# Modulation by rows of 128 outputs in the down phases of three networks, with narrower splits of the down weights

## The chip, the cores and the metric

The kernel runs on one core of one Trainium2 chip. A core has TensorE (matmul), VectorE, ScalarE and GpSimd, each with its own queue of instructions, and SyncE, which here only issues DMAs. The metric is device time in microseconds from first to last instruction as the runtime measures it. Three executions of the kernel before took 2091.39, 2093.84 and 2096.69 us.

## The reference

Two transformer blocks over x of 512 tokens by 1024 features, all in fp32. The first has a SwiGLU network, a mixer of attention, convolution and memory attention (mixA), and a second SwiGLU network. The second block has two layers; each has a mixer (mixB, an attention over selected keys; mixC, a short convolution) and a SwiGLU network of its own. In all: network 0, mixA, network 1, mixB, network 2, mixC, network 3. The second block's layers are modulated by a vector c:

```
c_act = jax.nn.silu(c)
for i in range(DEPTH_2):
    mod = c_act @ ada_w[i] + ada_b[i]              # (1, 6*1024)
    sh1, sc1, g1, sh2, sc2, g2 = split(mod, 6)
    h = _rmsnorm(x, norm1_g[i]) * (1.0 + sc1) + sh1
    x = x + g1 * mixer(h)
    h = _rmsnorm(x, norm2_g[i]) * (1.0 + sc2) + sh2
    x = x + g2 * _swiglu(h, w_gate[i], w_up[i], w_down[i])
```

ada_w is 2 x 1024 x 6144, 50.3 MB in fp32, read once and used for one vector only. It yields 12288 numbers, the tile modc of 128 partitions by 96 columns. From it come geff0 to geff3 (the norms' gains times 1 + scale), the shifts and the gates. They are first needed in the down phase of network 1.

## The kernel before, in words

**Matmuls.** Features lie on partitions, the 512 tokens on the free axis. Every fp32 matrix is held as a high and a low part (w_hi, w_lo and h_hi, h_lo), and each product is three matmuls, high x high, low x high, high x low (function product, L823 to L825), each 128x128 by 128x512.

**Jobs and the ring.** Weights come tile by tile, one tile a job, through a ring of four places. SyncE loads w_raw; ScalarE copies it to w_hi (split, L1392); VectorE subtracts to w_lo (split, L1917), or GpSimd does for most of the mixers' tiles (L720). Splits run LEAD = 3 jobs ahead of TensorE: in step s of a phase the engines split job s + 3. ScalarE's copy waits until TensorE has left the ring's place, VectorE's waits for ScalarE's, SyncE's next load for VectorE's.

**A network** has an up phase of 44 jobs (gate and up tiles of 1024 columns, 24 matmuls each) and a down phase of 32 jobs in four rounds of eight. A down job is a quarter of one output tile, of 6, 6, 5 or 5 blocks of 128 columns (DOWN_CUTS), though splits always work on all 1024 columns of a place. After every fourth job VectorE adds the result to x (update_x, L1939), ScalarE squares it, VectorE sums the squares (L1928) and splits the raw input of the next norm (raw_low, L1946).

**Modulation before.** It runs in the up phases of networks 0, 1 and 2, eight steps each of 512 outputs. For a step GpSimd loads four pieces of 512 KB of ada_w into the two places of ada_raw (ada_load, L689). VectorE takes the contraction over partitions and columns: one tensor_scalar and seven scalar_tensor_tensor into ada_sum (modulate), a transpose and a reduce (ada_partial), and GpSimd sends 8 KB through DRAM and back (ada_across), after which VectorE forms the total (ada_total).

**End of a down phase.** In the last round the splits are those of the following stage. GpSimd makes mixA's and mixB's low parts. In networks 1 and 2, shift_through (L1957, L1960) multiplies the mixer's first two weight tiles by the shift and sums over columns, eight operations a tile, on VectorE at steps 5 and 6. TensorE's first instruction of the mixer (first_two, L865) waits for the second one's sum, and then for the low part of the mixer's second tile. In network 1 the second tile has 8 columns a block.

Each engine works its queue strictly in order; what stands behind a waiting instruction waits as well.

## Time and profile before

| | |
|---|---|
| median of 3 runs | 2093.84 us |
| the profiled execution | 2091.56 us, span 2089.8 us |
| TensorE busy | 2071.9 us (99%), 10560 matmuls |
| VectorE busy | 1355.4 us (65%) |
| ScalarE busy | 862.9 us (41%) |
| GpSimd busy | 307.9 us (15%) |
| chain that ended last | PE 91%, DVE 6%, ACT 1% |
| DMA | 243.39 MB, mean 116 GB/s |
| granted TensorE clock | 1.00 |

In the profile PE is TensorE, DVE VectorE, ACT ScalarE, POOL GpSimd, SP SyncE; L1917 is line 1917 of the kernel. Matmuls overlap, and their ends are modelled: one of 512 columns is shown with 390 ns, but they start some 226 ns apart, so TensorE's pace is read from counts, not from busy time. A line may be a helper's: L1917 is every low split of VectorE. The down phases of networks 0, 1 and 2 lie at about 257 to 376, 808 to 928 and 1442 to 1561 us.

### The profile page before, as it was taken

How to read it: one execution, taken by the hardware profiler on the slowest of the kernel's cores; microseconds unless marked ns; L12 is line 12 of the kernel's file. 1: busy time of each engine (PE TensorE's matmuls, PEld its weight loads, DVE VectorE, ACT ScalarE, POOL GpSimd, SP SyncE). 2: the span in 40 equal slices, each digit the busy share in tenths (PEclk: the TensorE clock that was granted, in tenths of full speed). 3: DMA queues.
4: the chain of work that ended last, by engine and by line, in shares of the span. 5: the costliest groups of instructions: out<-in, count | busy, mean ns of one | idle time of the engine just before them, and what ended most of it. 6: DMA issues, size and time to landing. Idle time of an engine off the chain costs nothing.

```text
span 2089.8 us, 30098 instructions
## 1 busy us (share of the span) xinstructions
PE 2071.9 (99%) x10560; PEld 1730.1 (83%) x10560; DVE 1355.4 (65%) x1997; ACT 862.9 (41%) x1346; POOL 307.9 (15%) x369
## 2 busy tenths in 40 slices
PE   9999999999999999999999999999999999999999
PEld 8888888887888888877767888888888888999987
DVE  7666544787576654456997576664456459888832
ACT  6222233567442223334566342223333235455622
POOL 0121400660212221024320202220000000000000
PEclk9999999999999999999999999999999999999999
DMA  5556333330246542333310245642333222233332
GB/s 190 186 184 200 104 105 108 118 105 1 103 160 194 181 159 82 91 110 96 107 46 1 91 141 195 198 159 70 103 102 109 93 98 82 84 111 106 97 97 88
DMA packets 79578, 243.39 MB, mean 116 GB/s; under 512 B 12784, under 2 KB 13424, under 8 KB 79376
## 3 DMA queue, kind: packets, MB, share of 16 engines
q1 hardware_dynamic: 61376, 189.61, 27.8%
q0 software_dynamic: 18128, 52.84, 8.1%
q8 instruction: 42, 0.69, 0.1%
q14 instruction: 32, 0.26, 0.0%
HBM read 235.84 MB, written 2.29 MB: 114 GB/s over the span
## 4 chain that ended last, share of the span: by engine, by line
PE 91%; DVE 6%; ACT 1%; issue 1%; DMA 0%; SPq 0%; ACTq 0%; DVEq 0%
PE ps L823 25%; PE ps L825 25%; PE ps L824 25%; PE ps L919 3%; PE ps L918 3%; PE ps L917 3%; PE ps L1185 2%; DVE ps L2491 1%; PE ps L1167 1%; PE ps L1146 1%; DVE tmp L1960 1%; DVE small L2389 1%; PE ps L1309 0%; DVE ropA L2362 0%; DVE qA L2364 0%
## 5 line engine op out<-in xcount | busy, mean ns | idle before, releaser
L823 PE MATMUL ps<-h_hi,w_hi 128*128 128x512 f32 x1600 | 628.0, 392 | 2.2 <-issue 0.9
L825 PE MATMUL ps<-h_hi,w_lo 128*128 128x512 f32 x1600 | 623.0, 389 | 0.0
L824 PE MATMUL ps<-h_lo,w_hi 128*128 128x512 f32 x1600 | 622.7, 389 | 0.0
L1917 DVE TENSOR_TENSOR w_lo<-w_raw,w_hi 128x1024 fp32r<-128x1024 f32 x300 | 367.4, 1226 | 306.0 <-ACT w_hi L1392 293.6
L1392 ACT ACTIVATE w_hi<-w_raw 128x1024 fp32r<-128x1024 f32 x344 | 361.4, 1052 | 234.9 <-PE ps L825 233.1
L823 PEld LDWEIGHTS ps<-h_hi,w_hi 128*128 128x128 f32 x1600 | 299.6, 187 | 71.7 <-issue 8.2
L825 PEld LDWEIGHTS ps<-h_hi,w_lo 128*128 128x128 f32 x1600 | 299.5, 187 | 63.9
L824 PEld LDWEIGHTS ps<-h_lo,w_hi 128*128 128x128 f32 x1600 | 299.7, 187 | 61.9 <-issue 0.2
L823 PE MATMUL ps<-hid_hi,w_hi 128*128 128x512 f32 x704 | 274.0, 389 | 0.0
L824 PE MATMUL ps<-hid_lo,w_hi 128*128 128x512 f32 x704 | 273.9, 389 | 0.0
L825 PE MATMUL ps<-hid_hi,w_lo 128*128 128x512 f32 x704 | 273.9, 389 | 0.0
L720 POOL TENSOR_TENSOR w_lo<-w_raw,w_hi 128x512 fp32r<-128x512 f32 x100 | 133.6, 1356 | 447.3 <-ACT w_hi L1392 400.3
L1469 ACT ACTIVATE hid_hi<-tmp 128x512 f32 (+1 forms) x66 | 41.7, 632 | 293.2 <-DVE tmp L2097 287.1
L823 PEld LDWEIGHTS ps<-hid_hi,w_hi 128*128 128x128 f32 x704 | 132.1, 188 | 27.7 <-DVE hid_lo L2191 0.3
L824 PEld LDWEIGHTS ps<-hid_lo,w_hi 128*128 128x128 f32 x704 | 132.1, 188 | 27.4
L825 PEld LDWEIGHTS ps<-hid_hi,w_lo 128*128 128x128 f32 x704 | 132.1, 188 | 27.3
L2032 DVE SCALAR_TENSOR_TENSOR ada_sum<-ada_raw,c_act,ada_sum 128x512 f32<-128x512 f32 x168 | 125.9, 749 | 7.4 <-DMA ada_raw<-in_ada_w 3.1
L689 POOL DMA_DIRECT2D ada_raw<-in_ada_w x96 | 52.7, 549 | 393.6 <-DVE ada_sum L2032 372.7
L1466 ACT ACTIVATE tmp<-ps 128x512 f32<-128x512 f32 x62 | 37.1, 598 | 167.2 <-PE ps L825 167.2
L1402 ACT ACTIVATE tmp<-x 128x512 f32 (+1 forms) x56 | 35.3, 630 | 155.7 <-DVE x L1939 155.3
L2097 DVE TENSOR_TENSOR tmp<-tmp,ps 128x512 f32<-128x512 f32 x62 | 42.7, 688 | 78.0 <-PE ps L825 78.0
L2038 DVE TENSOR_TENSOR hid_lo<-tmp,hid_hi 128x512 f32 (+1 forms) x66 | 46.3, 701 | 57.4 <-ACT hid_hi L1469 57.4
(368 smaller groups left out, 2826.0 us busy)
## 6 DMA issues: line engine op xcount, KB each, us to landing
ada_raw<-in_ada_w POOLq DMA_DIRECT2D x96, 512.0 KB, 4.9
w_raw<-in_gate SPq DMA_DIRECT2D x88, 512.0 KB, 4.2
w_raw<-in_up SPq DMA_DIRECT2D x88, 512.0 KB, 3.5
w_raw<-in_down SPq DMA_DIRECT2D x64, 384.0 KB, 3.1
w_raw<-in_down SPq DMA_DIRECT2D x64, 320.0 KB, 2.9
w_raw<-in_w_mix_c SPq DMA_DIRECT2D x24, 512.0 KB, 3.5
w_raw<-in_w_mix_b SPq DMA_DIRECT2D x17, 512.0 KB, 3.5
w_raw<-in_w_mix SPq DMA_DIRECT2D x16, 512.0 KB, 3.5
```

What stands on the lines that cost most here:

```text
L689: pool.dma_start(ada_raw[:, (piece % 2) * 2 * ADA:(piece % 2 + 1) * 2 * ADA], src.rearrange("a p n -> (a p) n")).then_inc(ada_in[piece % 2 ...
L720: low = pool.tensor_tensor(w_lo[:, at:at + WT // 2], w_raw[:, at:at + WT // 2], f32(w_hi[:, at:at + WT // 2]), ALU.subtract)
L823: pe.matmul(dest, s_hi, m_hi, start=first and n == 0, stop=False)
L824: pe.matmul(dest, s_hi, m_lo, start=False, stop=False)
L825: mm = pe.matmul(dest, s_lo, m_hi, start=False, stop=last and n == len(pairs) - 1)
L917: pe.matmul(dest, w_hi[:, cut], m_hi, start=first and c == 0, stop=False, skip_group_check=not first)
L918: pe.matmul(dest, w_hi[:, cut], m_lo, start=False, stop=False, skip_group_check=not first)
L919: mm = pe.matmul(dest, w_lo[:, cut], m_hi, start=False, stop=c == KC // 2 - 1, skip_group_check=not first)
L1392: act.activation(chunk(w_hi, slot, WT), chunk(w_raw, slot, WT), ACT.Copy).then_inc(w_hi_done, 1)
L1917: dve.tensor_tensor(chunk(w_lo, slot, WT), chunk(w_raw, slot, WT), f32(chunk(w_hi, slot, WT)), ALU.subtract).then_inc(w_lo_done, 1)
L2032: dve.scalar_tensor_tensor(ada_sum[:, :], w, c_act[:, k:k + 1], ada_sum[:, :], ALU.mult, ALU.add).then_inc(ada_sum_done, 1)
L2038: dve.tensor_tensor(hid_lo[:, at], chunk(tmp, 2 + u), f32(hid_hi[:, at]), ALU.subtract)\
```

## The change

**Where and how modulation runs.** ada_w comes transposed, so that 128 outputs lie on partitions and the 1024 inputs along the free axis. One tensor_tensor_reduce (ada_row, L2046 after) multiplies a tile of 128x1024 by c_row, sums along the free axis, adds the bias and writes one column of modc; there is no transpose, reduce or trip through DRAM. It is built as two instructions: the multiply-and-sum and a small one that writes the sum. There are 32 rows in the down phase of each of networks 0, 1 and 2. ADA_AT says how many stand ahead of the split in each of a round's eight steps.

**Where the tiles lie.** Three places: slot 0 is the first half of ada_raw; slots 1 and 2, and c_row, lie in chunks 6, 5 and 7 of h_hi and h_lo, whose 512 columns each are free in a down phase until ScalarE writes the next norm's raw input there. So slot 2 is not used after row 25, nor slot 1 after row 29, and ADA_SLOTS ends in 0,1,0,1,0,0. GpSimd loads c_row and then row by row (ada_rows); a load waits until the row that last used its slot is done (ada_done).

**Other parts.** Splits of down weights cover 640 or 768 columns rather than 1024 (down_width). ScalarE's silu of c moves from the start of the kernel to each down phase, on 128x1024 (step 3). GpSimd makes the rope tables in the middle of an up phase, and ScalarE finishes them in step 2 of the down phase rather than ahead of it. The gains are formed in step 6 of the last round. VectorE's four rounds are written out, and one round each at ScalarE's two ends. Places and functions that choose others for network 2 if it were in SEVEN are not in use, as SEVEN is (3,) in both.

```diff
-ADA = 512
-ADA_STEPS = 2 * 6 * D // ADA
-ADA_PER_FFN = 8
+ADA_ROWS = 2 * 6 * KC
+ADA_PER_FFN = ADA_ROWS // 3
+ADA_AT = ((0, 0, 0, 0, 1, 1, 1, 1), (1, 2, 1, 1, 2, 2, 1, 1), (1, 2, 1, 1, 2, 2, 1, 1), (2, 1, 1, 1, 1, 0, 0, 0))
+ADA_SLOTS = (1, 2, 0) * 8 + (1, 2) + (0, 1, 0, 1, 0, 0)
...
+        over = h_over.rearrange("p (s k t) -> p s k t", s=2, k=KC)
+        c_row = over[:, :, KC - 1, :]
+        ada_tile = (ada_raw[:, 0:2 * T].rearrange("p (s t) -> p s t", s=2), over[:, :, KC - 2, :], over[:, :, KC - 3, :])
...
+        def down_width(s, by_parts, ends):
+
+            q = s + LEAD
+            if ends and q >= 8:
+                return WT
+            part = q // 2 if by_parts and q < 8 else q % 4
+            return (DOWN_CUTS[part + 1] - DOWN_CUTS[part]) * P
...
+            def ada_rows(n):
+
+                pool.wait_ge(job_done, first_job[f"ffn{n}"] + UP_JOBS + RING)
+                pool.dma_start(c_row, A["c_row"].rearrange("p (s t) -> p s t", s=2)).then_inc(c_in, 16)
+                for r in range(ADA_PER_FFN):
+                    slot = ADA_SLOTS[r]
+                    if ada_before(r) is not None:
+                        pool.wait_ge(ada_done, n * ADA_PER_FFN + ada_before(r) + 1)
+                    elif slot == 0 and n < 2:
+                        after(pool, a_misc, (("tabA", "tabB")[n], "cos"))
+                    elif slot == 0:
+                        pool.wait_ge(ada_done, n * ADA_PER_FFN)
+                    pool.dma_start(ada_tile[slot], A["ada_w"][n * ADA_PER_FFN + r].rearrange("p (s t) -> p s t", s=2))\
+                        .then_inc(ada_in[slot], 16)
...
+                def ada_row(r):
+
+                    at, slot = n * ADA_PER_FFN + r, ADA_SLOTS[r]
+                    dve.wait_ge(ada_in[slot], 16 * (ada_used(n, r) + 1))
+                    dve.wait_ge(c_ready, n + 1)
+                    dve.tensor_tensor_reduce(ada_tile[slot], ada_tile[slot], c_row, 1.0, col("ada_b", at), ALU.mult, ALU.add,
+                                             modc[:, at:at + 1]).then_inc(ada_done, 1)
...
-                def down(i, last, by_parts=False):
+                def down(i, last, by_parts=False, rows=(0,) * 8):
                     for s in range(8):
+                        for r in range(sum(rows[:s]), sum(rows[:s + 1])):
+                            ada_row(sum(sum(e) for e in ADA_AT[:i]) + r)
...
                         if last and n in (1, 2) and 8 - LEAD <= s < 10 - LEAD:
                             shift_through(2 * n + 1, s - (8 - LEAD))
                         if not (last and (n != 2 and s >= 8 - LEAD or s == 7)):
-                            split(J + UP_JOBS + s + LEAD, i, 8)
+                            split(J + UP_JOBS + s + LEAD, i, 8, down_width(s, by_parts, last))
```

**How the queues change.** VectorE, end of the last round of network 1's down phase, before: four splits, the block around update_x, one split, then shift_through.

```order
L1917 TENSOR_TENSOR w_lo<-w_raw,w_hi 128x1024 x4
L1939 SCALAR_TENSOR_TENSOR x<-ps,flat,x 128x512
L1928 TENSOR_TENSOR ssum<-ssum,tmp 128x512
L1946 SCALAR_TENSOR_TENSOR h_lo<-x,geff,h_hi 128x512
L1917 TENSOR_TENSOR w_lo<-w_raw,w_hi 128x1024
L1957 TENSOR_SCALAR tmp<-w_raw,modc 128x128
L1960 SCALAR_TENSOR_TENSOR tmp<-w_raw,modc,tmp 128x128 x7
L1957 TENSOR_SCALAR tmp<-w_raw,modc 128x8
L1960 SCALAR_TENSOR_TENSOR tmp<-w_raw,modc,tmp 128x8 x7
L1939 SCALAR_TENSOR_TENSOR x<-ps,flat,x 128x512
```

The same round after, from its first instruction to split 6 (rows 26 to 30; an ISA line with an input is the multiply-and-sum, `modc 128x1` its second instruction):

```order
L2046 ISA ada_raw,modc<-ada_raw,h_over,cols 128x1024
L2046 ISA modc 128x1
L2046 ISA h_over,modc<-h_over,cols 128x2x512
L2046 ISA modc 128x1
L1936 TENSOR_TENSOR w_lo<-w_raw,w_hi 128x640
L2046 ISA ada_raw,modc<-ada_raw,h_over,cols 128x1024
L2046 ISA modc 128x1
L1936 TENSOR_TENSOR w_lo<-w_raw,w_hi 128x768
L2046 ISA h_over,modc<-h_over,cols 128x2x512
L2046 ISA modc 128x1
L1936 TENSOR_TENSOR w_lo<-w_raw,w_hi 128x768
```

and from there to shift_through:

```order
L2046 ISA ada_raw,modc<-ada_raw,h_over,cols 128x1024
L2046 ISA modc 128x1
L1936 TENSOR_TENSOR w_lo<-w_raw,w_hi 128x640
L1957 SCALAR_TENSOR_TENSOR x<-ps,flat,x 128x512
L1946 TENSOR_TENSOR ssum<-ssum,tmp 128x512
L1964 SCALAR_TENSOR_TENSOR h_lo<-x,geff,h_hi 128x512
L2046 ISA ada_raw,modc<-ada_raw,h_over,cols 128x1024
L2046 ISA modc 128x1
L1936 TENSOR_TENSOR w_lo<-w_raw,w_hi 128x640
L1975 TENSOR_SCALAR tmp<-w_raw,modc 128x128
L1978 SCALAR_TENSOR_TENSOR tmp<-w_raw,modc,tmp 128x128 x7
```

Six rows now stand in front of shift_through, one of them (row 31) between the last update_x block and split 7. GpSimd's queue at the end of that series, in network 0, before: loads wait for ada_sum, and the trip through DRAM follows.

```order
L689 DMA ada_raw<-in_ada_w 128x1024 [waits ada_sum_done] x2
L696 DMA ada_room<-wi 128x16 [waits ada_done,ada_part_done]
L700 DMA wi<-ada_room 32x4x4 [waits ada_stored]
L700 DMA wi<-ada_room 32x4x4 x3
L729 DMA ada_raw<-in_positions 128x512 [waits ada_sum_done]
L738 CAST ada_raw<-ada_raw 128x512 [waits pos_in]
L740 ISA
```

After (h_over is where slots 1 and 2 lie): rows 24 to 31, each load waiting for an earlier row, then mixA's splits.

```order
L714 DMA h_over<-in_ada_w 128x2x512 [waits ada_done] x2
L714 DMA ada_raw<-in_ada_w 128x1024 [waits ada_done]
L714 DMA h_over<-in_ada_w 128x2x512 [waits ada_done]
L714 DMA ada_raw<-in_ada_w 128x1024 [waits ada_done]
L714 DMA h_over<-in_ada_w 128x2x512 [waits ada_done]
L714 DMA ada_raw<-in_ada_w 128x1024 [waits ada_done] x2
L725 TENSOR_TENSOR w_lo<-w_raw,w_hi 128x512 [waits w_lo_done,w_hi_done]
```

The splits that GpSimd owes to mixA now stand behind the last row's load, which waits for the row before it; before, they stood behind the rope tables.

## Rows read from the trace of the kernel before

**Rows 1.** Stages: busy us (instructions) by engine, clock, DMA share, GB/s.
```profile
50.00:250.00 200.00, 200.00 (x884) 165.62 (x883) 126.72 (x170) 59.42 (x76) 44.28 (x76) 1.00 0.55 178
250.00:370.00 120.00, 120.00 (x532) 99.34 (x530) 53.82 (x56) 43.13 (x50) 13.60 (x11) 1.00 0.33 100
...
1650.00:1700.00 50.00, 50.00 (x222) 41.27 (x221) 23.29 (x28) 12.57 (x15) 0.00 (x0) 1.00 0.29 97
```

**Rows 2.** Waits of TensorE: total us, times, longest us.
```profile
PE ps L1146 <- ACT pB L1708: 2.2, 4, 1.1
...
PE ps L865 <- DVE tmp L1960: 1.2, 1, 1.2
```

**Rows 3.** Groups by shape: busy us, mean ns, idle before and releaser.
```profile
L1917 DVE TENSOR_TENSOR w_lo<-w_raw,w_hi 128x1024 fp32r<-128x1024 f32 x300 | 367.4, 1226 | 306.0 <-ACT w_hi L1392 293.6 <-ACT w_hi L1752 6.2 <-ACT w_hi L1570 0.5
...
L2032 DVE SCALAR_TENSOR_TENSOR ada_sum<-ada_raw,c_act,ada_sum 128x512 f32<-128x512 f32 x168 | 125.9, 749 | 7.4 <-DMA ada_raw<-in_ada_w 3.1
...
L2044 DVE STREAM_TRANSPOSE ada_turned<-ada_sum 128x512 f32<-128x512 f32 x24 | 16.9, 705 | 0.0
L1939 DVE SCALAR_TENSOR_TENSOR x<-ps,modc,x 128x512 f32<-128x512 f32 x22 | 16.5, 749 | 29.6 <-PE ps L825 29.6
L2046 DVE TENSOR_REDUCE wi<-ada_turned 128x16 f32<-128x512 f32 x24 | 16.5, 686 | 0.8
...
L2029 DVE TENSOR_SCALAR ada_sum<-ada_raw,c_act 128x512 f32<-128x512 f32 x24 | 11.5, 481 | 0.0
```

**Rows 4.** VectorE in order of time, network 1's last round: start us, duration us.
```profile
898.13 0.75 DVE L1939 SCALAR_TENSOR_TENSOR x<-ps,flat,x 128x512 f32 x1 [1.31 <-PE ps L825]
899.85 0.69 DVE L1928 TENSOR_TENSOR ssum<-ssum,tmp 128x512 f32<-128x512 f32 x1 [0.96 <-ACT tmp L1402]
...
901.32 1.23 DVE L1917 TENSOR_TENSOR w_lo<-w_raw,w_hi 128x1024 fp32r<-128x1024 f32 x1
...
918.04 0.28 DVE L1957 TENSOR_SCALAR tmp<-w_raw,modc 128x128 f32<-128x128 f32 x1 [0.77 <-ACT w_hi L1392]
918.36 6.54 DVE L1960 SCALAR_TENSOR_TENSOR tmp<-w_raw,modc,tmp 128x128 f32<-128x128 f32 x7
...
925.07 3.83 DVE L1960 SCALAR_TENSOR_TENSOR tmp<-w_raw,modc,tmp 128x8 f32<-128x8 f32 x7
928.82 0.74 DVE L1939 SCALAR_TENSOR_TENSOR x<-ps,flat,x 128x512 f32<-128x512 f32 x1
...
933.56 0.18 DVE L1967 RECIPROCAL token_rstd<-token_std 128x4 f32<-128x4 f32 x1 [1.75 <-ACT token_std L1414]
```

**Rows 5.** TensorE at the end of that round.
```profile
927.40 0.39 PE L825 MATMUL ps<-hid_hi,w_lo 128*128 128x512 f32 x1
928.96 0.38 PE L865 MATMUL ps<-ones,tmp 128*128 128x1 f32 x2 [1.18 <-DVE tmp L1960]
```

**Rows 6.** VectorE at the end of network 2's down phase.
```profile
1551.85 0.29 DVE L1957 TENSOR_SCALAR tmp<-w_raw,modc 128x128 f32<-128x128 f32 x1 [0.76 <-ACT w_hi L1392]
1552.17 2.68 DVE L1960 SCALAR_TENSOR_TENSOR tmp<-w_raw,modc,tmp 128x128 f32<-128x128 f32 x7
1554.77 1.22 DVE L1917 TENSOR_TENSOR w_lo<-w_raw,w_hi 128x1024 fp32r<-128x1024 f32 x1
```

**Rows 7.** The stage table for the first 9 us of weights and x.
```profile
2.00:11.00 9.00, 8.20 (x58) 8.01 (x56) 3.06 (x4) 4.26 (x9) 0.00 (x0) 1.00 0.99 345
```

**Rows 8.** Loads of ada_raw, from issue to landing.
```profile
DMA to landing us min/median/max: 3.8/4.9/7.1
```

**Rows 9.** All engines, an up phase: VectorE's release and GpSimd's issue.
```profile
116.00 1.53 DVE L2032 SCALAR_TENSOR_TENSOR ada_sum<-ada_raw,c_act,ada_sum 128x512 f32<-128x512 f32 x2
...
117.83 0.53 POOL L689 DMA_DIRECT2D ada_raw<-in_ada_w  x1 [5.83 <-DVE ada_sum L2032]
```

**Rows 10.** GpSimd beside VectorE's rows 4.
```profile
918.09 2.68 POOL L720 TENSOR_TENSOR w_lo<-w_raw,w_hi 128x512 fp32r<-128x512 f32 x2 [125.93 <-ACT w_hi L1392]
...
925.56 2.53 POOL L720 TENSOR_TENSOR w_lo<-w_raw,w_hi 128x512 fp32r<-128x512 f32 x2 [0.81 <-ACT w_hi L1392]
```

More of the change, by code:

```diff
@@ L267, in build, with ada_used, ada_before @@
         SHIFTED = range(3, 7)
-        def ada_from(n):
-            return 2 if n == 0 else 1
+        def ada_used(n, r):
+            slot = ADA_SLOTS[r]
+            return n * ADA_SLOTS.count(slot) + ADA_SLOTS[:r].count(slot)
+        def ada_before(r):
+            same = [q for q in range(r) if ADA_SLOTS[q] == ADA_SLOTS[r]]
+            return same[-1] if same else None
         def raw_halves(n):
@@ L583, in fresh @@
         def fresh(n, k, ring):
-            return chunk(h_whole, k) if n % 2 == 0 and n // 2 in SEVEN else chunk(tmp, k % ring)
+            return chunk(places(n // 2)[6], k) if n % 2 == 0 and n // 2 in SEVEN else chunk(tmp, k % ring)
         block = ctx.enter_context(nc.Block())
@@ L1204, in _ @@
             idle(30)
-            pe.wait_ge(prep, 1)
             ffn(0)
@@ L1594, in units, with down @@
                     unit(UNITS // 2 - 1, 1, last=True)
-                def down(i, last, by_parts=False):
+                def down(i, last, by_parts=False, first=False, ends=False):
                     for s in range(8):
                         if not (last and s >= 8 - LEAD):
-                            split(J + UP_JOBS + s + LEAD, i, 8)
+                            split(J + UP_JOBS + s + LEAD, i, 8, down_width(s, by_parts, ends))
+                        if first and s == 2 and n < 2:
+                            tables(("tabA", "tabB")[n], col(("sign_a", "sign_b")[n]))
+                        if first and s == 3:
+                            act.wait_ge(c_in, 16 * (n + 1))
+                            act.activation(c_row, c_row, ACT.Silu).then_inc(c_ready, 1)
                         if by_parts and s < 4:
@@ L1604, in down @@
                                 hidden_high(u)
-                        if s % 4 == 3 and n < 3:
+                        if by_parts and n < 3 and s >= 6:
+                            square_x(2 * n + 1, s - 6, s - 6)
+                            raw_high(s - 6, next_gain)
+                        if s % 4 == 3 and n < 3 and not by_parts:
                             square_x(2 * n + 1, i * 2 + s // 4, s // 4)
@@ L1615, in ffn @@
                 if n in (1, 2):
-                    after(act, d_misc, f"geff{2 * n - 1}")
-                if n < 2:
-                    tables(("tabA", "tabB")[n], col(("sign_a", "sign_b")[n]))
+                    after(act, d_misc, f"geff{2 * n - 2}")
                 if n < 3:
-                    with act.Fori(0, KC // 2) as i:
+                    down(0, False, by_parts=n in SEVEN, first=True)
+                    with act.Fori(1, KC // 2 - 1) as i:
                         down(i, False)
+                    down(KC // 2 - 1, False, ends=True)
                 else:
@@ L1912, in _, with split @@
         def _(dve):
-            def split(first, i=0, step=4):
+            def split(first, i=0, step=4, width=WT):
                 slot = first % RING
+                cut = slice(slot * WT, slot * WT + width)
                 dve.wait_ge(w_hi_done, i * step + (first + 1))
-                dve.tensor_tensor(chunk(w_lo, slot, WT), chunk(w_raw, slot, WT), f32(chunk(w_hi, slot, WT)),
-                                  ALU.subtract).then_inc(w_lo_done, 1)
+                dve.tensor_tensor(w_lo[:, cut], w_raw[:, cut], f32(w_hi[:, cut]), ALU.subtract).then_inc(w_lo_done, 1)
             def lead(first, i=0, step=4):
@@ L2065, in up @@
                         u = s // 2
-                        if modulation:
-                            for k in range(2 * s, 2 * s + 2):
-                                modulate(i + (n * ADA_PER_FFN - ada_from(n)), k)
-                            if totals and s == 3:
-                                ada_total(i + (n * ADA_PER_FFN - ada_from(n) - 1))
                         raw = first and u < RAW_PAIRS.get(2 * n, 0)
@@ L2786, in layout @@
     a["w_out_c"] = tiles(g["conv_w_out_2"][0])
-    ada = np.concatenate([tiles(g["ada_w_2"][l], ADA) for l in range(2)], axis=0)
-    ada = ada.reshape(ADA_STEPS, P, KC, 4, 4, 32).transpose(0, 1, 2, 4, 3, 5)
-    a["ada_w"] = np.ascontiguousarray(ada).reshape(ADA_STEPS, P, KC * ADA)
+    ada = [np.asarray(g["ada_w_2"][l]).T for l in range(2)]
+    a["ada_w"] = np.ascontiguousarray(np.concatenate(ada, axis=0)).reshape(ADA_ROWS, P, D)
+    a["c_row"] = np.ascontiguousarray(np.broadcast_to(g["c_2"].reshape(1, D), (P, D)))
     return a
```

197 lines of the change are left out of this document (79 added, 118 removed).

## The prediction, made before the changed kernel ran

> **What bounds the kernel now.** I read the stage table first [rows 1], then the engines' waits [rows 2], the groups of instructions by shape [rows 3], and last the two ends of a down phase in order of time [rows 4, 5, 6]. The stage table says almost everything about the upside. In an up phase with modulation TensorE takes 884 matmuls of 512 columns in 200 us, 226.2 ns each, at granted clock 1.00; in mixC, which has no modulation, it takes 222 in 50 us, which is the same pace within half a per cent; in a down phase it takes 532 in 120 us, again the same. TensorE is back to back in all of them, and the change takes none of its 10560 matmuls away. VectorE is busy for only 127 of 200 us in an up phase and 57 of 120 us in a down phase. So taking VectorE work out of an up phase buys nothing by itself. The longest single wait of TensorE in the stretches that the change touches is the 1.2 us behind shift_through in front of mixB [rows 2, 5]. All that can be won there is about that; what can be lost is a new wait, in a down phase that becomes full.
>
> **The parts.** Time is told from T, the start of the last round of eight down jobs. A round is 132 matmuls x 226.2 ns = 29.9 us; jobs have 18, 18, 15, 15 matmuls (4.07 or 3.39 us). In network 1 the last matmul of the round starts at 927.40 [rows 5], so T = 927.6 - 29.9 = 897.7.
>
> Removed from each of three up phases: eight steps of one tensor_scalar (0.48), seven scalar_tensor_tensor (0.75), one transpose (0.71) and one reduce (0.69) [rows 3]: 7.1 us x 8 = 57 us of VectorE per network, and the round trip of partial sums through DRAM. It lies beside TensorE that never waits: worth 0. Also c_act's 0.2 us on ScalarE at the start, in idle time: 0.
>
> Narrower splits: VectorE's low half of 1024 columns takes 1.226 us [rows 3], a tensor_tensor of 512 takes 0.69 [rows 4], so 768 columns take 0.96 and 640 take 0.83. A round's eight splits fall from 9.8 to 7.2 us on VectorE; ScalarE saves about as much. Nothing waits for these splits today (each is ready three jobs ahead), so they are worth 0 alone, but they pay for part of what comes in.
>
> Added: 32 rows per down phase, 4, 11, 11 and 6 by round. A row is one multiply-and-sum over 128x1024 with both inputs in SBUF, and a small instruction that reads the sum out. The trace has no such pair. Below, it costs what a plain 128x1024 tensor_tensor costs, 1.23 us; above, twice that and a small operation, 2.45 us. The nearest rows are the tensor_tensor and, for an operation with little in it, the 0.18 us reciprocal [rows 3, 4]; I take 1.4 us, since the removed scalar_tensor_tensor with two SBUF inputs takes 0.75 us for 512 columns, exactly as long as the update of x, whose one input is PSUM [rows 3]. So two SBUF inputs alone do not slow this engine down. The Trainium skill, "Vector Engine (DVE) Microarchitecture Reference", section "Points that are easy to get wrong", says that scalar_tensor_tensor with two SBUF sources that are not bf16 runs at half rate, because no read port is left for the accumulator. The trace contradicts it for the form without a sum, and no row shows the form with one; it is rival D below.
>
> VectorE's account of a middle round: 11 rows x 1.4 = 15.4, splits 7.2, and twice the block around update_x, which in the trace lasts from 898.13 to 901.32 with its two waits for ScalarE [rows 4], 3.2 each: 29.0 us of 29.9. It fits, with 3% to spare.
>
> DMA account of a middle round: 11 rows of 0.524 MB and 2.88 MB of weights, 8.65 MB in 29.9 us = 289 GB/s. The trace's densest stretch, the first 9 us, moved 345 GB/s at a share of 0.99 [rows 7]. It fits too, at 84%; the down phase moves 100 GB/s today [rows 1].
>
> **The new wait.** A row waits for its 512 KB. GpSimd issues the load once the row that last used the place is done, and everything of VectorE's queue stands behind a row that hasn't landed: the next split (which TensorE and, through the ring, SyncE's next weight load wait for), update_x, shift_through. A load of this size took 3.8 us at least, 4.9 median, 7.1 at most from issue to landing [rows 8]; VectorE's finish to GpSimd's issue is 0.3 us (116.00 + 1.53 to 117.83) [rows 9]. With 0.1 to wake, a place turns around in 5.3 us and then needs 1.4 for its row. In the middle rounds three places serve a row every (5.3 + 1.4) / 3 = 2.2 us, and 2.7 are given. But in the last round h_hi's places are being given back, and the slots read 0,1,0,1,0,0: row 28 waits for 26's place, 30 for 28's, 31 for 30's. Three turnarounds in series.
>
> Walk it. The block around update_x ends at T+3.6 (901.3). Row 26 runs 3.6 to 5.0. Row 28 can't start before 10.3, ends 11.7. Row 30 starts 17.0, ends 18.4. Split 6 and the block of update_x fit in meanwhile. Row 31 starts 23.7, ends 25.1; split 7 ends at 25.9. TensorE wants split 7 when job 7 starts, T+26.5: 0.6 us to spare. In network 0 nothing else follows, so it loses nothing.
>
> In networks 1 and 2 shift_through stands behind split 7, and TensorE's first matmul of the mixer waits for it. Before, it started at T+20.3 (918.04) and ended at 928.9, T+31.2; now it starts at T+25.9. In network 1 its operations took 6.54 us / 7 = 0.93 each, for GpSimd was splitting weights at the same time [rows 10]; in network 2, with GpSimd silent, 2.68 / 7 = 0.38 [rows 6]. GpSimd's splits end at T+30.4 as before. So five of the eight wide ones run slow until 30.4, three fast ones take 1.2, the eight narrow ones, 0.55 each in the trace, perhaps 0.3 (estimated by the same ratio): end at T+34.0. Network 1 loses 34.0 - 31.2 = 2.8 us. Bounds: 0 to 5.6.
>
> In network 2 the queue after split 7 is shift 3.0, split 1.2, shift 3.0, split 1.2 [rows 6]: 25.9 + 8.4 = T+34.3, where TensorE is ready at T+29.9 (before, the queue got there in time: both shifts began at T+20.3 and the waits list nothing). It loses 4.4 us. Bounds: 0 to 6.
>
> A middle round at 97% of VectorE and with two rows in one job four times a round will not come out exactly on time; I put 0.5 us of lateness at T, which network 0 still absorbs and the others pay in full. Sum: 0 + 3.3 + 4.9 = 8.2 us. The profiled execution took 2091.56 (span 2089.8 and 1.8 around it): 2099.8. The median of the runs shown is 2.3 above the profiled one, so against it the sum is 2102.0. I say 2101.
>
> The Trainium skill, "DMA: Bandwidth & Descriptors", section "Anatomy of one DMA — SWDGE (gpsimd) path", fits a GpSimd-issued DMA as 2.0 us plus its bytes at 436 GB/s. By that 512 KB land in 3.2 us, the three turnarounds shrink by 5 us in total, and the loss falls to nearly nothing. The trace's shortest is 3.8 and its median 4.9 [rows 8], so it does not agree here, and the sum goes by the rows.
>
> **The rivals.**
> A (forecast): 4.9 us landings, rows of 1.4 us, +8.2 us.
> B: no measurable loss. The last round moves only six rows in 20 us, so its loads may run nearer to the minimum of 3.8 than to a median taken while gate and up weights moved too. Turnaround 4.2: row 31 ends at T+21.8, split 7 at 22.6, shift_through starts 2.3 us later than before; network 1 loses at most 2.3, network 2: 22.6 + 8.4 = 31.0, that is 1.1. Sum 1 to 3.4 us: 2093 to 2097. It decides from a landing of about 4.2 us on. Against it: 84% load just before, and destinations of two 2 KB pieces in the h_hi places.
> C: the load itself slows its transfers, 6 us landings (inside the range of rows 8). Each of three turnarounds is 1.1 longer, and (6.4 + 1.4) / 3 = 2.6 per row nearly fills the 2.7, so pairs of rows wait and some 1.5 us of lateness arrives at T. Per network 4.8 more: 4.2 in network 0 after its 0.6 of slack, 7.6 and 9.2 in the others: +21 us, 2114.
> D: the multiply-and-sum runs at half rate, 2.45 us. A middle round is 27 + 7.2 + 6.4 = 40.6 us of VectorE in 29.9, 10.7 late, twice; the last round's six rows, splits and block up to shift_through are 26 against 20.3; less the 5 or so us by which splits are early. 22 us a network, +65: 2158. TensorE would then wait in the middle rounds.
> E: faster. Only the 1.2 us wait in front of mixB is there to be won, and only if VectorE came to shift_through sooner, which w_hi of that job (918.0) forbids. The narrower splits could do what the title says and nothing else.
>
> **Chances.** A 0.45 (its own range 2097 to 2109), B 0.33, C 0.09, D 0.10, E 0.03. What a measurement can tell from no change is 0.3%, 6.3 us, so B and the low end of A (0.07) are "within": 0.40. Slower: the rest of A, C and D, 0.57. Faster by more than 0.3% would need five times the stall there is: 0.03. Range: 2091 to 2120, which leaves out D and the tails.
>
> **What would show it.** In the profile after: up phases at 884 matmuls per 200 us with VectorE near half busy; the row's main instruction 1.2 to 1.5 us (D: above 2.2); landings of in_ada_w 4.5 to 5.5; VectorE idle before three rows of the last round, released by a DMA; shift_through starting some 5 us later, and TensorE waits of 3 to 5 us in front of mixB and mixC, none in front of mixA. Wrong, if TensorE waits within the middle rounds, if the waits for DMA are absent, or if anything in the up phases gets shorter.

## The result and the profile after

The changed kernel took 2109.01 us, median of 4 runs (2107.17 to 2111.14), and the kernel before, beside it, 2094.48 (2091.39 to 2096.69). The ratio is 1.0071 with a 95% interval of 1.0053 to 1.0088: slower by 0.7%, clear of the noise. The profiled execution took 2108.0 us with a span of 2106.2, that is 16.4 us longer than the span of before.

The page of the changed kernel: busy times, then groups (line, engine, operation, tiles; busy us and mean ns; idle before and its releaser), then DMA issues with the median us to landing.

```profile
PE 2079.3 (99%) x10560; PEld 1734.4 (82%) x10560; DVE 1264.7 (60%) x1901; ACT 834.0 (40%) x1348; POOL 256.8 (12%) x252
...
PE 81%; DVE 10%; DMA 5%; issue 3%; ACT 1%; SPq 0%; ACTq 0%; POOL 0%; DVEq 0%; POOLq 0%
...
L2046 DVE CUSTOM_DVE_ANT_1 h_over<-h_over,cols 128x1024 f32<-128x1024 f32 x60 | 76.6, 1280 | 26.9 <-DMA h_over<-in_ada_w 26.8
...
h_over<-in_ada_w POOLq DMA_DIRECT2D x60, 512.0 KB, 5.9
...
ada_raw<-in_ada_w POOLq DMA_DIRECT2D x36, 512.0 KB, 5.8
```

VectorE's busy time fell by 90.7 us and GpSimd's by 51.1, and the kernel is slower. Ahead of the last instruction the chain now holds 10% VectorE and 5% DMA. One row is 1280 ns, and the loads land in 5.9 us where they took 4.9 [rows 8].

The stage table, the stretches of [rows 1] (the down phase is the second):

```profile
50.00:250.00 200.00, 200.00 (x884) 165.68 (x883) 74.01 (x75) 59.45 (x76) 15.95 (x12) 1.00 0.30 97
250.00:370.00 120.00, 118.84 (x525) 98.11 (x523) 78.73 (x116) 36.80 (x51) 21.93 (x33) 1.00 0.69 235
1650.00:1700.00 50.00, 50.00 (x222) 41.40 (x221) 22.94 (x27) 12.57 (x15) 0.00 (x0) 1.00 0.29 97
```

The up phase lost 53 of its 127 us of VectorE and has the same 884 matmuls. The down phase has 525 matmuls instead of 532: the losses are there.

The waits of TensorE (total us, times, longest) that answer to [rows 2]:

```profile
PE ps L871 <- DVE tmp L1978: 8.5, 2, 5.2
PE ps L829 <- DVE w_lo L1936: 2.8, 2, 2.3
```

L871 is L865 of before. In front of mixB TensorE waits 5.2 us (before 1.2), in front of mixC 3.3 and 0.5 more (before 0), and at network 0's last down job 2.3 (before 0). Together 10.1 us more. What happened in network 1's last round on VectorE, where [rows 4] show before:

```profile
906.77 1.28 DVE L2046 CUSTOM_DVE_ANT_1 ada_raw<-ada_raw,h_over,cols 128x1024 f32<-128x1024 f32 x1
907.97 0.08 DVE L2046 DVE_READ_ACCUMULATOR2_ANT modc<- 128x1 f32 x1
...
912.17 1.28 DVE L2046 CUSTOM_DVE_ANT_1 ada_raw<-ada_raw,h_over,cols 128x1024 f32<-128x1024 f32 x1 [2.17 <-DMA ada_raw<-in_ada_w]
...
919.18 1.28 DVE L2046 CUSTOM_DVE_ANT_1 ada_raw<-ada_raw,h_over,cols 128x1024 f32<-128x1024 f32 x1 [0.80 <-DMA ada_raw<-in_ada_w]
...
924.83 1.28 DVE L2046 CUSTOM_DVE_ANT_1 ada_raw<-ada_raw,h_over,cols 128x1024 f32<-128x1024 f32 x1 [0.89 <-DMA ada_raw<-in_ada_w]
...
926.78 0.28 DVE L1975 TENSOR_SCALAR tmp<-w_raw,modc 128x128 f32<-128x128 f32 x1
927.09 8.44 DVE L1978 SCALAR_TENSOR_TENSOR tmp<-w_raw,modc,tmp 128x128 f32<-128x128 f32 x7
...
935.87 1.80 DVE L1978 SCALAR_TENSOR_TENSOR tmp<-w_raw,modc,tmp 128x8 f32<-128x8 f32 x7
```

These are rows 26, 28, 30 and 31, then shift_through. GpSimd and TensorE at the same time, for [rows 10] and [rows 5]:

```profile
927.01 7.99 POOL L725 TENSOR_TENSOR w_lo<-w_raw,w_hi 128x512 fp32r<-128x512 f32 x6 [5.69 <-DVE w_lo L1936]
```

```profile
932.09 0.39 PE L831 MATMUL ps<-hid_hi,w_lo 128*128 128x512 f32 x1
937.72 0.71 PE L871 MATMUL ps<-ones,tmp 128*128 128x1 f32 x4 [5.25 <-DVE tmp L1978]
938.37 0.80 PE L829 MATMUL ps<-h_hi,w_hi 128*128 128x512 f32 x1
938.96 0.63 PE L830 MATMUL ps<-h_lo,w_hi 128*128 128x512 f32 x1
939.39 0.63 PE L831 MATMUL ps<-h_hi,w_lo 128*128 128x512 f32 x1
```

The reader is to see three things. The last matmul of the round starts at 932.09, so T = 932.3 - 29.9 = 902.4, and row 31 starts at T+22.4. GpSimd, which before split a tile, paused and split the next [rows 10], now stands until VectorE's split 7 is done and then does all six pieces without a gap, so each of the seven wide operations of shift_through runs beside it and takes 1.2 us; in network 2, where GpSimd is silent, seven take 2.67. The narrow ones, behind GpSimd's last piece, are shorter in return (1.80 us, in [rows 4] 3.83): from its first instruction to its last sum shift_through takes 10.9 us, as before, and the 4.1 us by which it starts later (T+24.4 for T+20.3) are the 4.1 us that the wait grew. And after the wait the matmuls start 0.43 us apart, not 0.23. The stage table says why: the granted clock (the last column but two).

```profile
930.00:933.00 3.00, 2.48 (x11) 1.70 (x10) 2.93 (x3) 0.24 (x1) 2.86 (x3) 1.00 0.00 0
933.00:936.00 3.00, 0.00 (x0) 0.00 (x0) 2.89 (x7) 0.00 (x0) 2.00 (x2) 0.81 0.01 3
936.00:939.00 3.00, 1.28 (x6) 1.14 (x7) 2.12 (x8) 0.64 (x2) 0.37 (x1) 0.50 0.70 191
939.00:942.00 3.00, 3.00 (x9) 1.72 (x8) 1.37 (x2) 2.09 (x3) 0.18 (x1) 0.55 0.93 351
942.00:945.00 3.00, 3.00 (x19) 2.07 (x17) 0.18 (x1) 1.21 (x2) 0.00 (x0) 1.00 0.18 72
```

While TensorE stands, its clock goes from 2.4 to 1.2 GHz, and it is still there for some 4 us after the wait ends: 9 matmuls in 3 us, then 19. The same follows the waits in networks 0 and 2 (0.65 in 373 to 376, 0.60 in 1576 to 1579). Before, the clock is 1.00 all through its profiled span. So 10.1 of the 16.4 us are waits, and most of the other 6.3 come with the slower clock behind them. Matching the 10560 matmuls of the two traces in order checks this by place: the changed kernel gains 1.1 us in its first 20 us, then loses 5.0 at network 0's last job, 0.8 up to the end of network 1, 5.8 in front of mixB and 6.0 around the start of mixC. The three places lose 16.8 us, 10.1 of them waits. The clock is also down once in mixB's attention (0.97 in 1050 to 1100 us), which by the same count costs nothing in the end.

### The profile page after: what moved, and what is told of

Same layout as the page of the kernel before. It is cut to its first block, busy times and chain, and to the rows that moved or that the text cites. A ratio compares the mean times of both kernels' runs of the same rounds, so it can differ in the third digit from the quotient of the medians.

```text
span 2106.2 us, 29456 instructions
## 1 busy us (share of the span) xinstructions
PE 2079.3 (99%) x10560; PEld 1734.4 (82%) x10560; DVE 1264.7 (60%) x1901; ACT 834.0 (40%) x1348; POOL 256.8 (12%) x252
## 4 chain that ended last, share of the span: by engine, by line
PE 81%; DVE 10%; DMA 5%; issue 3%; ACT 1%; SPq 0%; ACTq 0%; POOL 0%; DVEq 0%; POOLq 0%
PE ps L829 22%; PE ps L831 22%; PE ps L830 22%; DMA h_over<-in_ada_w 3%; PE ps L926 3%; PE ps L925 3%; PE ps L924 3%; PE ps L1192 2%; DMA ada_raw<-in_ada_w 2%; DVE ps L2486 1%; PE ps L1174 1%; DVE w_lo L1936 1%; DVE h_over L2046 1%; PE ps L1153 1%; DVE tmp L1978 1%
## 5 line engine op out<-in xcount | busy, mean ns | idle before, releaser
L1936 DVE TENSOR_TENSOR w_lo<-w_raw,w_hi 128x1024 fp32r<-128x1024 f32 (+2 forms) x300 | 329.7, 1099 | 311.5 <-ACT w_hi L1399 299.6
L1399 ACT ACTIVATE w_hi<-w_raw 128x1024 fp32r<-128x1024 f32 (+2 forms) x344 | 329.8, 962 | 247.5 <-PE ps L831 244.7
L2046 DVE CUSTOM_DVE_ANT_1 h_over<-h_over,cols 128x1024 f32<-128x1024 f32 x60 | 76.6, 1280 | 26.9 <-DMA h_over<-in_ada_w 26.8
L924 PE MATMUL ps<-t_hi,w_hi 128*128 128x256 f32 x288 | 81.5, 283 | 0.0
L925 PE MATMUL ps<-t_lo,w_hi 128*128 128x256 f32 x288 | 81.5, 283 | 0.0
```

Of the source, the lines that this page charges most:

```text
L924: pe.matmul(dest, w_hi[:, cut], m_hi, start=first and c == 0, stop=False, skip_group_check=not first)
L925: pe.matmul(dest, w_hi[:, cut], m_lo, start=False, stop=False, skip_group_check=not first)
L1399: act.activation(w_hi[:, cut], w_raw[:, cut], ACT.Copy).then_inc(w_hi_done, 1)
L1936: dve.tensor_tensor(w_lo[:, cut], w_raw[:, cut], f32(w_hi[:, cut]), ALU.subtract).then_inc(w_lo_done, 1)
L2046: dve.tensor_tensor_reduce(ada_tile[slot], ada_tile[slot], c_row, 1.0, col("ada_b", at), ALU.mult, ALU.add, modc[:, at:at + 1]).then_inc(a ...
```

## The experiments

The theory after the result: (1) rows and turnarounds of a place in series make the last round's end late on VectorE; (2) GpSimd's splits run beside shift_through, so it takes its full 10.9 us and the late start reaches TensorE whole; (3) TensorE's clock falls in the waits and adds half as much again. Rivals: VectorE is simply too full; the load of the DMAs itself slows the clock; the narrower splits or the lighter up phases have effects of their own. Letters of theories are those of each expectation's own text. Ratios are to the kernel before, run beside each.

**The narrower splits alone**, in the kernel before:

```diff
+        def down_width(s, by_parts, ends):
...
+                            split(J + UP_JOBS + s + LEAD, i, 8, down_width(s, by_parts, ends))
```

> The kernel before with the narrower splits of down weights alone, modulation as before in the up phases. My sum priced them at 0, as each split is ready three jobs ahead: 2092 to 2096 us, same waits in front of mixB. Rival: shorter splits let something start sooner at a phase's end, 1 to 3 us faster.

2092.8 us, ratio 1.0001 (0.999 to 1.0012). Worth nothing alone, as priced.

**Most loads taken away**, all arithmetic kept:

```diff
                     if ada_before(r) is not None:
-                        pool.wait_ge(ada_done, n * ADA_PER_FFN + ada_before(r) + 1)
+                        continue
```

> The changed kernel with the loads of rows 3 to 31 of each network left out: the multiply-and-sums run all the same, on what lies in the three places (so modc is not the reference's). VectorE's work is as it was, only the waits for loads and their traffic are gone. Theory S: no row waits, 2092 to 2097 us, TensorE's waits as in the kernel before, clock 1.000. Theory V in its form 'VectorE is too full' (29 us of 29.9 in a middle round): at least half of the loss stays, 2101 us or more.

2094.19 us, ratio 1.0005 (0.9994 to 1.0016). Rows 3 to 31 compute on old data and nothing is lost. VectorE is not too full: 32 rows and their splits fit.

**All loads kept, half the arithmetic**:

```diff
-                    dve.tensor_tensor_reduce(ada_tile[slot], ada_tile[slot], c_row, 1.0, col("ada_b", at), ALU.mult, ALU.add,
+                    dve.tensor_tensor_reduce(ada_tile[slot][:, 0], ada_tile[slot][:, 0], c_row[:, 0], 1.0, col("ada_b", at), ALU.mult, ALU.add,
```

> The changed kernel with all of its loads at their places and sizes, but each row multiplies and sums only 512 of its 1024 columns (half of each sum is left out). A row then takes about 0.65 us of VectorE instead of 1.28. Theory L (VectorE waits for loads; its own time matters little): a middle round has 6 us more of idle, the three turnarounds in series shorten by 3 x 0.6 = 2 us only, and most of the loss stays: 2099 to 2106. Rival V (the down phase is simply too full of VectorE work): the loss is gone, 2092 to 2096.

2094.26 us, ratio 1.0008 (0.9996 to 1.002). I expected most of the loss to stay, and it went: theory L falls as I put it. Yet rival V can't be right either, since the kernel without loads has the full arithmetic and loses nothing. VectorE's waits for these DMAs, in us, times, longest:

```profile
DVE h_over L2046 <- DMA h_over<-in_ada_w: 30.2, 21, 2.9
DVE ada_raw L2046 <- DMA ada_raw<-in_ada_w: 23.8, 18, 2.8
```

They are 54.0 us, more than the 46.5 of the changed kernel (26.8 and 19.7), and cost nothing. So neither the waits nor the work is the cause by itself, but their sum on one chain: a row is inside each turnaround. VectorE in network 1 here, rows 26, 28, 30, 31 and the start of shift_through:

```profile
899.56 0.75 DVE L2046 CUSTOM_DVE_ANT_0 ada_raw<-ada_raw,h_over,cols 128x512 f32<-128x512 f32 x1
...
904.46 0.75 DVE L2046 CUSTOM_DVE_ANT_0 ada_raw<-ada_raw,h_over,cols 128x512 f32<-128x512 f32 x1 [2.73 <-DMA ada_raw<-in_ada_w]
...
909.83 0.75 DVE L2046 CUSTOM_DVE_ANT_0 ada_raw<-ada_raw,h_over,cols 128x512 f32<-128x512 f32 x1 [0.89 <-DMA ada_raw<-in_ada_w]
...
914.86 0.75 DVE L2046 CUSTOM_DVE_ANT_0 ada_raw<-ada_raw,h_over,cols 128x512 f32<-128x512 f32 x1 [0.43 <-DMA ada_raw<-in_ada_w]
...
916.84 0.29 DVE L1975 TENSOR_SCALAR tmp<-w_raw,modc 128x128 f32<-128x128 f32 x1 [0.49 <-ACT w_hi L1399]
```

From row 26 to row 31 it is 15.3 us, against 18.1 in the changed kernel (906.77 to 924.83). Of these 2.8 us 1.6 are the three shorter rows and 1.2 a landing that happened to be shorter. Another 1.3 us come from the start: with T at 896.5 here, row 26 starts at T+3.1 and not at T+4.4, so the middle rounds hand on less lateness. With row 31 done early, shift_through waits for ScalarE's w_hi again, as in [rows 4], and not for a row.

**Three loads of the last round taken away**, rows 28, 30 and 31:

```diff
+                    if r in (28, 30, 31):
+                        continue
```

> The changed kernel, but rows 28, 30 and 31 of each network multiply what lies in the place instead of loading their own 512 KB (their outputs are therefore left out). All other loads, all arithmetic and the order of VectorE stay. Theory S (the three turnarounds of one place in series are what makes shift_through late): the waits in front of mixA, mixB and mixC fall to 0.5, 1.5 and 0 us and the time is 2091 to 2096. Rival M (lateness piled up in the middle rounds and by row 29's load): half of the loss or more stays, 2100 to 2107.

2097.1 us, ratio 1.0023 (1.0013 to 1.0034), in between the two. Nine loads fewer of 96 take some two thirds of the loss away; the chain is the main cause. In its profiled execution (2095.13 us) the waits of 10.1 us are down to 1.6: TensorE waits 2.8 us in front of mixB (before 1.2) and no longer in front of mixA and mixC. In network 1, TensorE's last matmul of the round and its wait, then VectorE's row 26 and shift_through:

```profile
925.98 0.39 PE L835 MATMUL ps<-hid_hi,w_lo 128*128 128x512 f32 x1
929.12 0.51 PE L875 MATMUL ps<-ones,tmp 128*128 128x1 f32 x4 [2.75 <-DVE tmp L1982]
```

```profile
902.02 1.28 DVE L2052 CUSTOM_DVE_ANT_1 ada_raw<-ada_raw,h_over,cols 128x1024 f32<-128x1024 f32 x1
...
918.02 0.28 DVE L1979 TENSOR_SCALAR tmp<-w_raw,modc 128x128 f32<-128x128 f32 x1
918.33 8.60 DVE L1982 SCALAR_TENSOR_TENSOR tmp<-w_raw,modc,tmp 128x128 f32<-128x128 f32 x7
...
927.26 1.80 DVE L1982 SCALAR_TENSOR_TENSOR tmp<-w_raw,modc,tmp 128x8 f32<-128x8 f32 x7
```

shift_through starts at the same time as in [rows 4], but TensorE is earlier here: T is 896.3, so this is T+21.7 and not T+20.3. Row 26 starts at T+5.7, so part of rival M is right: about 1.4 us of lateness from the middle rounds come through. The wide operations take 8.60 us where [rows 4] have 6.54, as GpSimd waits for split 7 and then runs beside them,

```profile
918.26 5.32 POOL L729 TENSOR_TENSOR w_lo<-w_raw,w_hi 128x512 fp32r<-128x512 f32 x4 [12.72 <-DVE w_lo L1940]
```

but the narrow ones take 1.80 where they had 3.83, and the whole is 11.0 us against 10.9. The rest of this execution's loss is a low clock in mixB's attention (0.90 in 1050 to 1100 us); whether that belongs to the change is not shown.

**The splits at full width** beside the rows:

```diff
             q = s + LEAD
-            if ends and q >= 8:
-                return WT
-            part = q // 2 if by_parts and q < 8 else q % 4
-            return (DOWN_CUTS[part + 1] - DOWN_CUTS[part]) * P
+            return WT
```

> The changed kernel with all splits of down weights at 1024 columns as before. A middle round of VectorE is then 11 x 1.21 + 8 x 1.14 + 6.4 = 28.8 us of 29.9 by the pitches now measured, instead of 26.3, and each row's wait for its load comes on top. Theory F (the narrower splits pay for the waits of the middle rounds): some 2.5 us per round arrive late, the last round starts late, 2113 to 2125. Rival N (they are worth nothing even beside the rows, since VectorE idles for loads anyway): 2107 to 2111.

2112.43 us, ratio 1.0099 (1.0085 to 1.0114). That is 3.4 us above the changed kernel by the medians and 5.9 by the ratios, with intervals that overlap slightly; in the traces TensorE's waits for splits and for shift_through are 15.0 us instead of 11.3, the one in front of mixB 6.7 instead of 5.2. So worth nothing alone, the narrower splits probably pay for 3 to 6 us here. The time lies between rival N and theory F.

**No rows at all**:

```diff
-                for r in range(ADA_PER_FFN):
+                for r in range(0):
...
-                            ada_row(sum(sum(e) for e in ADA_AT[:i]) + r)
+                            pass
```

> The changed kernel without any modulation: no load of ada_w or c_row, no rows, no silu of c (modc is set to zero, so what depends on it is left out of the output). It keeps the lighter up phases and the narrower splits. Theory U (up phases and splits give nothing back, as TensorE never waited there): 2090 to 2093, up phases still 884 matmuls per 200 us. Rival G (there is a gain from the removed up-phase work which the down phases' loss hides): 2080 to 2087.

2091.51 us, ratio 0.9991 (0.9981 to 1.0). Taking the whole modulation out is worth at most 4 us, 2.3 by the medians. So if the up phases hold a gain, it is smaller than that, and far from rival G's.

**A delay alone**, in the kernel before, ahead of shift_through:

```diff
+                        if last and n in (1, 2) and s == 8 - LEAD:
+                            delay(9)
```

> The kernel before, with nothing of the change in it; nine scalar_tensor_tensor of 128x512 on a scratch tile (about 6.5 us of VectorE) stand ahead of shift_through in the last rounds of networks 1 and 2. There are no loads and no rows in the down phases. Theory V (a late shift_through is all it takes, and TensorE's lower clock follows from the wait): TensorE waits 3 to 5 us in front of mixB and 4 to 5 us in front of mixC, the granted clock falls to 0.5 for some us right behind each, and the time is 2092 + 7 to 9 us of waits + 3 to 5 us of slow clock = 2102 to 2106. Rival W (the clock fell in the changed kernel for another reason, such as its DMAs): the same waits, clock 1.0 behind them, 2099 to 2101.

2106.62 us, ratio 1.0072 (1.0054 to 1.0089): the change's whole loss, without any of the change. TensorE waits 9.6 us, 6.7 of them in front of mixB, and the clock is down behind it though the DMAs move nothing while TensorE stands (first line; the last column is GB/s):

```profile
930.00:933.00 3.00, 0.00 (x0) 0.00 (x0) 2.72 (x10) 0.00 (x0) 0.00 (x0) 0.80 0.00 0
933.00:936.00 3.00, 1.80 (x7) 1.56 (x8) 1.98 (x7) 0.98 (x2) 0.63 (x1) 0.50 0.74 233
936.00:939.00 3.00, 3.00 (x10) 1.50 (x8) 1.05 (x2) 1.75 (x3) 0.00 (x0) 0.57 0.98 343
939.00:942.00 3.00, 3.00 (x20) 2.24 (x19) 0.18 (x1) 1.21 (x2) 0.28 (x1) 1.00 0.09 36
```

Theory V holds, with a time just above its range; rival W doesn't. The delay was meant to be equal in both networks and was not. VectorE in networks 1 and 2:

```profile
916.95 12.30 DVE L1954 SCALAR_TENSOR_TENSOR ada_sum<-x 128x512 f32<-128x512 f32 x9
...
1558.36 6.50 DVE L1954 SCALAR_TENSOR_TENSOR ada_sum<-x 128x512 f32<-128x512 f32 x9
```

The same nine operations take 12.3 us beside GpSimd's splits and 6.5 alone, so the waits are 6.7 and 2.9 us, where 3 to 5 and 4 to 5 were expected.

**The waits filled**: the changed kernel, with TensorE at work on nothing.

```diff
+                    if n in (3, 5):
+                        idle(30 if n == 3 else 20)
                     after(pe, shift_acc, (n, 1, KC - 1))
```

> The changed kernel, with TensorE given matmuls of 128x128 on a tile of ones while it would stand in front of mixB (30 of them) and of mixC (20); in the trace 78 of these take 12.0 us, so they fill 4.6 and 3.1 us of waits of 5.2 and 3.3. Their result is overwritten. Theory K (the clock falls because TensorE stands still): the granted clock stays at 1.0 behind both waits, VectorE is late as before, and the time is 2109 less 3 to 5 us, 2104 to 2106; the wait of 2.3 us in front of mixA and what follows it are left. Rival R (the clock falls for another reason, and the fillers only take their time): the clock is 0.5 behind both, 2109 to 2111.

2105.54 us, ratio 1.006 (1.0041 to 1.0079), 3.5 us below the changed kernel by the medians of two sets, 2.3 by the ratios. The clock behind the wait in front of mixB is:

```profile
930.00:933.00 3.00, 3.00 (x22) 2.73 (x21) 2.93 (x3) 0.00 (x0) 2.86 (x3) 1.00 0.01 3
933.00:936.00 3.00, 3.00 (x29) 3.00 (x28) 2.75 (x11) 0.00 (x0) 0.60 (x1) 1.00 0.26 68
936.00:939.00 3.00, 3.00 (x27) 2.91 (x26) 2.26 (x5) 2.02 (x3) 0.55 (x1) 1.00 0.81 277
```

VectorE is about as late as before (shift_through starts at T+23.8) and the clock stays up, in front of mixC too: theory K. The intervals of the two ratios overlap, so the times alone don't show it; the clock does. The fillers are more than was needed: in this trace they take 6.9 us in front of mixB and 4.6 in front of mixC and end 1.9 and 1.0 us after the sums were ready. Three of the six executions have a granted clock of 1.000 and took 2102.3 to 2103.4 us; executions of the kernel before beside them at 0.999 or 1.000 took 2090.6 to 2091.6. That is 12 us: 11.5 of fillers in place of a wait of 1.2, and 1.8 of waiting in network 0.

**Row 31 two steps later**, behind the first tile of shift_through:

```diff
-..., (2, 1, 1, 1, 1, 0, 0, 0))
+..., (2, 1, 1, 1, 0, 0, 1, 0))
```

> Of the changed kernel only the last round's table differs: row 31 stands at step 6 of the round and no longer at step 4, behind split 7 and the first half of shift_through. Theory S (the loss sits in the series 26, 28, 30, 31 of loads into one place): split 7 now waits for row 30 alone, so TensorE's 2.3 us wait inside network 0's last round goes, shift_through starts within 2 us of where it did before, the waits in front of mixB and mixC fall from 8.5 us to under 3, and 2094 to 2099 us come out. Theory V (VectorE and the DMA engines are simply too full over the whole down phase): one row moved by two steps changes nothing that counts, 2106 to 2111 us. Theory K (of some 17 us, 7 are TensorE's clock at its lower level behind each long wait): with the waits the low stretches go too, mean granted clock from 0.996 to 1.000; if the clock falls for another reason, it stays at 0.996 or below.

2105.05 us, ratio 1.0063 (1.0045 to 1.008), with the widest spread of all, 2096.61 to 2111.0, and the profiled execution was the fastest of them. The median lies outside both ranges. In that execution shift_through starts at T+21.6, row 31 now stands inside it and takes 2.30 us beside GpSimd's split, and TensorE waits 3.8 us in front of mixB, 0.5 in mixC and not at all in front of mixA. So it shows less than the median lost. Where the slower ones lost it, perhaps to row 28's or 29's loads, was not seen and stays open. It shows that one row's place is not enough.

**Rows moved from the last round to the first** as well:

```diff
-ADA_AT = ((0, 0, 0, 0, 1, 1, 1, 1), ..., (2, 1, 1, 1, 1, 0, 0, 0))
+ADA_AT = ((0, 0, 0, 0, 1, 1, 2, 2), ..., (1, 1, 1, 0, 0, 0, 1, 0))
```

> The changed kernel with ADA_AT = ((0,0,0,0,1,1,2,2), (1,2,1,1,2,2,1,1), (1,2,1,1,2,2,1,1), (1,1,1,0,0,0,1,0)): two rows more in the first round, four in the last, row 31 again at step 6. Theory S: rows 28 and 30 stand at steps 0 and 2, so nothing of the series reaches split 7; TensorE's waits in network 0 and in front of mixC go altogether, in front of mixB 1 to 2 us stay: 2093 to 2096 us. Theory V: two rows more in a round with eight splits and the tables make that round late; no better than row 31 alone moved.

2095.39 us, ratio 1.0012 (1.0003 to 1.0022). With four rows in the last round instead of six nearly all is won back; what is left is a wait of 2.7 us in front of mixB, with the clock at 0.50 from 930 to 936 us behind it. shift_through starts on time (T+20.4), and row 31 stands inside it.

**GpSimd held**, from that kernel, row 31 at step 5:

```diff
+            after(pool, shift_acc, (3, 0, KC - 1))
             for j in range(LEAD):
                 split(first_job["mixB"] + j)
```

> Rows spread differently: round 0 has 6 (two ahead of each of the last two splits), the last round 4, at steps 0, 1, 2 and 5, so that row 31 is done before shift_through; and GpSimd's first split of mixB waits until shift_through is done with the first tile. Theory P (in the last round of network 1 VectorE is slowed by GpSimd's splits beside it, 0.93 against 0.38 us per operation): the eight wide operations take about 3.0 us, shift_through ends before TensorE is ready, the wait in front of mixB is 0 to 0.5 us instead of 1.2 to 2.7, and the time is 2089 to 2092. Rival Q (GpSimd's splits, now some 3 us later, are what TensorE waits for in mixB instead): 2093 to 2097.

2095.82 us, ratio 1.0012 (1.0003 to 1.0021). The wide tile took what was expected, and the narrow one gave it back, on VectorE:

```profile
917.58 2.68 DVE L1979 SCALAR_TENSOR_TENSOR tmp<-w_raw,modc,tmp 128x128 f32<-128x128 f32 x7
...
921.70 6.57 DVE L1979 SCALAR_TENSOR_TENSOR tmp<-w_raw,modc,tmp 128x8 f32<-128x8 f32 x7
```

Eight columns or 128, an operation beside GpSimd took 0.94 us. The wait in front of mixB was 1.4 us, about that of before the change. Neither theory had this. The profiled execution took 2090.82 us, the second fastest of twelve, so it doesn't show what the median's 3 us are; the executions above 2092 us had mean clocks of 0.994 to 0.998.

**GpSimd held twice**: splits 2 and 3 too.

```diff
-            after(pool, shift_acc, (3, 0, KC - 1))
             for j in range(LEAD):
+                after(pool, shift_acc, (3, min(j, 1), KC - 1))
                 split(first_job["mixB"] + j)
```

> As the kernel with GpSimd's first split of mixB held, but its second and third are held too, until shift_through is done with the second, narrow tile. Theory P (a VectorE operation beside a GpSimd split takes 0.9 to 1.2 us whatever its width, so the narrow ones cost as much as the wide ones): of the seven narrow operations only the first few run beside the first split, they take about 3.5 instead of 6.6 us together, TensorE's wait for shift_through is gone, and it waits 0 to 1 us for GpSimd's second split instead: 2090 to 2094, no better than the kernel before by more than 1 us. Rival Q (the held splits make mixB's third tile late): a wait for GpSimd of 1.5 us or more, 2095 to 2099.

2092.45 us, ratio 0.9992 (0.9982 to 1.0001). The seven narrow operations took 2.78 us, and TensorE's wait for shift_through is gone (900 to 950 us: busy 50.00). It has all of the change and loses nothing. Its median is 1.3 us below that of before, within what the interval leaves open: not shown to be faster. The profiled execution was the slowest of the eleven, 2099.13 us, with the clock down in mixB's attention (0.83 in 1050 to 1100 us, 0.66 in 1150 to 1170) and no long wait ahead of it. The four executions at a mean clock of 0.999 or 1.000 took 2088.7 to 2089.4 us, where seven of the kernel before took 2090.5 to 2092.0: at an equal clock it looks 2 us faster, but that comparison was chosen after the fact.

## Why the prediction came out as it did

The sign and the mechanism were right, and two of the three places; the time was 8 us short of 2109.0 and inside the range. The time alone doesn't speak for the forecast: it lies on the upper edge of A's own range and is nearer to C's 2114. The trace does: the waits grew by 2.3, 4.1 and 3.8 us, where A had 0, 3.3 and 4.9 and C 4.2, 7.6 and 9.2. By its own steps:

- **What bounds the kernel.** Right: the up phases still have 884 matmuls in 200 us, and the kernel without rows is at 0.9991.
- **The row.** 1.28 us and a sum read of 0.08, at a pitch of 1.21 (906.77 to 907.97), against 1.4. Rival D, the half rate, is out: 1280 ns for 1024 columns is 4% above a plain tensor_tensor of that size [rows 3], 750 for the 512 of the half-arithmetic kernel 9% above the 0.69 us of [rows 4].
- **The account of a middle round.** It fits, and TensorE doesn't wait there. The lateness at T in network 1 was 0.8 us (906.77 is T+4.4, said was T+3.6), against 0.5.
- **The turnaround.** The landings were 5.9 us at the median, with 7.5 at most, against 4.9; rival C's figure of 6 was nearer. Two terms were loose: no row shows the 0.1 us to wake, and [rows 8] hold every transfer into ada_raw. The loads of ada_w alone took 4.1 us at least, 4.9 at the median and 7.1 at most, so the 3.8 on which rival B leaned was not one of them. From the end of a row to the start of the next in that place it was 4.1, 5.7 and 4.4 us in network 1, against 5.3. So the last round's chain went a little faster than walked: rows 28, 30 and 31 started at T+9.8, 16.8 and 22.4 in network 1 (said: 10.3, 17.0, 23.7). In networks 0 and 2 row 31's load took 7.4 us and it started at T+26.7 and T+24.3. The chain has no average: three draws from 3.7 to 7.5 us.
- **Network 0.** Wrong, and the prediction had said that there would be no wait in front of mixA: 0.6 us of slack were taken to hold, and row 31's long landing turned them into a wait of 2.3 us. TensorE was ready at 368.8, which is T+26.5. VectorE of the changed kernel there, start and duration:

```profile
361.24 0.82 DVE L1936 TENSOR_TENSOR w_lo<-w_raw,w_hi 128x640 fp32r<-128x640 f32 x1
...
369.02 1.28 DVE L2046 CUSTOM_DVE_ANT_1 ada_raw<-ada_raw,h_over,cols 128x1024 f32<-128x1024 f32 x1 [4.22 <-DMA ada_raw<-in_ada_w]
370.23 0.08 DVE L2046 DVE_READ_ACCUMULATOR2_ANT modc<- 128x1 f32 x1
370.23 0.82 DVE L1936 TENSOR_TENSOR w_lo<-w_raw,w_hi 128x640 fp32r<-128x640 f32 x1
```

- **Network 1.** 3.3 us said, 4.1 measured, by two errors of opposite sign. shift_through started earlier than walked (T+24.4, not 25.9), but "GpSimd's splits end at T+30.4 as before" failed: they wait for VectorE's split 7, which is behind row 31, and ran from 927.0 to 935.0, T+32.6, without a gap. The walk moved an instruction on VectorE and forgot who waits for it on GpSimd.
- **Network 2.** 4.9 said, 3.8 measured.
- **The sum.** Waits: 8.2 said, 10.1 measured. The term that was missing is the clock, some 6 us. It was 1.00 throughout in the profiled execution of before; the delay alone and the filled waits show it to be a consequence of TensorE's standing still. The prediction had no such term, so that the range still held the result was width and not insight.
- **Rival B**, short landings, was given 0.33. Against it stood the load of the DMAs in the middle rounds. The landings did get longer and not shorter; that the load is the reason fits (the down phase moved 235 GB/s for 100), but no run isolates it.
